# The first run of matmuls takes six weight tiles instead of four, with its weights loaded chunk by chunk into three raw buffers

## The reference

```python
def rmsnorm(x, g):
    xf = x.astype(jnp.float32)
    y = xf * lax.rsqrt(jnp.mean(xf * xf, axis=-1, keepdims=True) + EPS)
    return (y * g.astype(jnp.float32)).astype(x.dtype)

def swiglu(x, w_gate, w_up, w_down):
    return (jax.nn.silu(x @ w_gate) * (x @ w_up)) @ w_down

def first_block(x, meta_tokens, ffn1_norm, ffn1_w_gate, ffn1_w_up, ffn1_w_down, ...):
    meta = jnp.broadcast_to(meta_tokens.astype(x.dtype)[None], (B, N_META, D_MODEL))
    h = jnp.concatenate([meta, x], axis=1)
    for l in range(DEPTH):
        h = h + 0.5 * swiglu(rmsnorm(h, ffn1_norm[l]), ffn1_w_gate[l], ffn1_w_up[l], ffn1_w_down[l])
        proj = rmsnorm(h, mix_norm[l]) @ w_in[l]
        ...                                     # retention and differential attention, w_out
        h = h + 0.5 * swiglu(rmsnorm(h, ffn2_norm[l]), ffn2_w_gate[l], ffn2_w_up[l], ffn2_w_down[l])
    h = rmsnorm(h, final_norm)
    return h[:, N_META:]

# second_block: SwiGLU, short convolution, SwiGLU, SwiGLU, dilated attention, SwiGLU, each behind an rmsnorm
```

## Time and profile before

| | |
|---|---|
| median of three runs | 2173.55 us (2172.53 to 2174.04) |
| the profiled execution | 2174.74 us |
| its span, first to last instruction | 2172.9 us |
| TensorE busy | 2161.8 us, 99% of the span |
| VectorE busy | 1558.9 us, 72% |
| ScalarE busy | 1221.3 us, 56% |
| GpSimd busy | 461.5 us, 21% |
| chain that ended last | TensorE 92%, DVE 4%, ACT 2%, DMA 1%, issue 1% |
| mean granted TensorE clock | 0.948 |

### The profile page before, as it was taken

The page is one execution under the profiler, slowest core; times in us unless marked ns, Lnnn a source line. Parts: engine busy times, 40 slices in busy tenths (PEclk is TensorE's granted clock), DMA queues, the critical chain, the costliest instruction groups (busy, mean ns, idle before and its releaser), DMA issues.

```text
span 2172.9 us, 38658 instructions
## 1 busy us (share of the span) xinstructions
PE 2161.8 (99%) x15616; PEld 2040.9 (94%) x15616; DVE 1558.9 (72%) x2589; ACT 1221.3 (56%) x2020; POOL 461.5 (21%) x500
## 2 busy tenths in 40 slices
PE   9999999999999999999999999999999999999999
PEld 9999999999999999988988999889888999999888
DVE  7655876765665586886697586975876688887863
ACT  6444465544544446665566545654655666676652
POOL 1000522420341052232053000430321011101420
PEclk9999999999999999999999999999999999999999
DMA  9655434975785543565566554755565566674653
GB/s 277 202 170 171 155 121 133 235 197 174 190 213 175 183 156 117 163 206 184 165 211 199 191 179 152 233 185 191 186 194 175 170 194 171 175 236 139 225 178 105
DMA packets 425680, 395.34 MB, mean 182 GB/s; under 512 B 16559, under 2 KB 421935, under 8 KB 425504
## 3 DMA queue, kind: packets, MB, share of 16 engines
q1 hardware_dynamic: 411856, 375.01, 55.3%
q0 software_dynamic: 13360, 17.61, 3.9%
q10 hardware_dynamic: 288, 0.27, 0.0%
HBM read 389.20 MB, written 7.41 MB: 183 GB/s over the span
## 4 chain that ended last, share of the span: by engine, by line
PE 92%; DVE 4%; ACT 2%; DMA 1%; issue 1%; SPq 0%; DVEq 0%; ACTq 0%
PE ps L1663 29%; PE ps L1659 25%; PE ps L1661 16%; PE ps L1662 16%; DVE t L1155 2%; PE ps L1982 1%; PE ps L1980 1%; PE ps L1981 1%; DMA t<-attn_w_qkv 1%; ACT t L830 0%; PE ps L1948 0%; PE ps L1932 0%; PE ps L1961 0%; DMA t<-ffn_w_up 0%; PE ps L1758 0%
## 5 line engine op out<-in xcount | busy, mean ns | idle before, releaser
L1663 PE MATMUL ps<-t 128*128 128x256 f32 (+1 forms) x5504 | 1562.2, 284 | 0.0
L1663 PEld LDWEIGHTS ps<-t 128*128 128x128 f32 x5504 | 1038.4, 189 | 0.1
L1155 DVE TENSOR_TENSOR t<-t 128x1024 fp32r<-128x1024 f32 (+1 forms) x724 | 879.0, 1230 | 175.8 <-ACT t L830 175.3
L1661 PE MATMUL ps<-t 128*128 128x272 f32 (+1 forms) x3084 | 890.3, 289 | 1.0 <-DVE t L1618 0.8
L830 ACT ACTIVATE t<-t 128x1024 fp32r<-128x1024 f32 (+1 forms) x724 | 732.1, 1030 | 265.8 <-PE ps L1663 234.4
L1662 PE MATMUL ps<-t 128*128 128x272 f32 (+1 forms) x3084 | 879.8, 285 | 0.0
L1659 PE MATMUL ps<-t 128*128 128x512 f32 x2420 | 840.4, 390 | 0.1
L1661 PEld LDWEIGHTS ps<-t 128*128 128x128 f32 x3084 | 580.9, 188 | 7.6 <-issue 3.9
L1662 PEld LDWEIGHTS ps<-t 128*128 128x128 f32 x3084 | 583.7, 189 | 1.0
L1659 PEld LDWEIGHTS ps<-t 128*128 128x128 f32 x2420 | 454.2, 188 | 95.3 <-DVE t L1155 0.4
L754 POOL TENSOR_TENSOR t<-t 128x256 f32<-128x256 f32 x110 | 100.2, 910 | 694.0 <-ACT t L946 694.0
(11 more groups left out here) (198 smaller groups left out, 1535.3 us busy)
## 6 DMA issues: line engine op xcount, KB each, us to landing
t<-ffn_w_in SPq DMA_DIRECT2D x88, 1024.0 KB, 5.4
t<-ffn_w_gate SPq DMA_DIRECT2D x42, 1024.0 KB, 5.5
t<-ffn_w_up SPq DMA_DIRECT2D x42, 1024.0 KB, 7.4
t<-attn_w_qkv SPq DMA_DIRECT2D x72, 512.0 KB, 5.0
t<-ffn_w_down SPq DMA_DIRECT2D x32, 1024.0 KB, 5.3
t<-ffn_w_out SPq DMA_DIRECT2D x32, 1024.0 KB, 5.3
t<-w_in SPq DMA_DIRECT2D x28, 1024.0 KB, 5.1
t<-ffn_w_down SPq DMA_DIRECT2D x16, 768.0 KB, 4.4
```

Source lines behind the costliest of these rows:

```text
L1155: dve.tensor_tensor(wlo[:, plan.place[n], 0:nk, :], raw[:, u % NRAW, 0:nk, half * P:half * P + P], f32(whi[:, plan.place[n], 0:nk, :]), AL ...
L1661: pe.matmul(o, hi, xhi, start=i == 0, stop=False)
L1663: ins = pe.matmul(o, lo, xhi, start=False, stop=i == r.nk - 1)
```

## The change

The first run takes six tiles. Its weights are two units of 384 columns, gate and up. They lie in raw buffers 0 to 2, which are seen as eight chunks of 768 columns, and are loaded chunk by chunk with the residual: 24 loads on SP in the place of 13. The two units behind them (tiles 6 and 7) are 128 columns wide and share raw buffer 3. The gains of stage 0 (eight columns) come by a small load of their own ahead of the rest of `vec`. GpSimd loads no part of `h`. DVE makes the high x of chunk 0, ACT that of the other seven, and the two tables of `vec` are made behind all of this. TensorE has its own procedure for the first run (`project_first`): for chunk 0 it does the high by high matmuls of all six tiles, then high by low, then low by high, each group behind its own semaphores; for each other chunk three matmuls a tile as before. Each tile of the run reports its own end (`spent`). The matmul of the norm stays ahead of chunk 5 of the run behind the first, which is now that of tile 6 and was that of tile 4. TensorE does four matmuls without use in the place of five.

```diff
-FIRST = [(0, 1), (1, 2), (2, 4), (4, 6), (6, 8)]
-WARM = 5
+NFIRST = 6
+WARM = 4
...
-                for n in [4] + [1] * (2 * FCH - 4):
+                n = 4 if s else NFIRST
+                for n in [n] + [1] * (2 * FCH - n):
                     self.run(s, n, KC, c0, range(8))
...
+        cols = range(0, F, PAIR)
+        if not self.order:
+            each = NFIRST // 2
+            firsts = [self.unit(w, 0, 8, first, each * P) for w, first in (gate, up)]
+            self.order += [(u, i) for i in range(each) for u in firsts]
+            self.order += [(self.unit(w, 0, 8, first + each * P, P), 0) for w, first in (gate, up)]
+            cols = range(each * P + P, F, PAIR)
+        for c in cols:
+            self.weights_pair(gate[0], gate[1] + c, up[0], up[1] + c)
...
-            self.spent += [mm + i + 1 if i < r.rounds - 1 else mm + i + n] * n
+            last = [mm + 1 + j for j in range(n)] if first == 0 else [mm + i + n] * n
+            self.spent += [mm + i + 1] * n if i < r.rounds - 1 else last
...
+        raw_first = raw[:, 0:3, :, :].rearrange("p r k n -> p (r k n)").rearrange(
+            "p (k u c) -> p k u c", k=KC, u=2)
...
+        def kept(u):
+            if u < NRAW:
+                return raw[:, 3, :, (u - 2) * P:(u - 1) * P]
+            return raw[:, u % NRAW, :, :]
...
             load_first(sp, 0, 1)
-            sp.dma_start(vec[:, :], A["vec"]).then_inc(S["vec"], 16)
...
+            sp.dma_start(vec[:, V_FFN1:V_FFN1 + KC], A["vec"][:, V_FFN1:V_FFN1 + KC]).then_inc(S["gains"], 16)
+            for k in range(1, KC):
+                load_residual(sp, k)
+                load_first(sp, k, 0)
+                load_first(sp, k, 1)
+                if k == 2:
+                    sp.dma_start(vec[:, KC:], A["vec"][:, KC:]).then_inc(S["vec"], 16)
...
                 if u >= NRAW:
-                    w.wait_ge(S["lo"], plan.last[u - NRAW] + 1)
+                    w.wait_ge(S["lo"], max(plan.last[u - NRAW] + 1, NFIRST))
...
+            w.wait_ge(S["gains"], 16)
+            for k in range(KC):
+                if k:
+                    high_x(0, k)
+                w.wait_ge(S[f"first{k}"], 32)
+                ins = act.activation(first_pieces(whi, k), first_pieces(raw, k), ACT.Copy)
+                ins.then_inc(*((S["hi_first"], 1) if k < KC - 1 else (S["hi"], NFIRST)))
+            hi.up(NFIRST)
             w.wait_ge(S["vec"], 16)
             w.wait_ge(S["set"], 1)
...
+            w.wait_ge(S["gains"], 16)
+            w.wait_ge(S["h0"], 16)
+            dve.tensor_scalar(x[:, 0, 0, :], h[:, 0, :], gain(0, 0), None, ALU.mult).then_inc(S["xh"], 1)
+            for k in range(KC):
+                low_x(0, k)
+                w.wait_ge(*((S["hi_first"], k + 1) if k < KC - 1 else (S["hi"], NFIRST)))
+                ins = dve.tensor_tensor(first_pieces(wlo, k), first_pieces(raw, k), f32(first_pieces(whi, k)), ALU.subtract)
...
+            def project_first(r):
+                def product(part, k, j):
+                    wt, m = ((whi, 0), (whi, 1), (wlo, 0))[part]
+                    return pe.matmul(ps[:, r.banks[j], 0:T], wt[:, plan.place[j], k, :], x[:, k, m, :],
+                                     start=(part, k) == (0, 0), stop=(part, k) == (2, KC - 1))
+                for part, sems in enumerate((("xh", "hi_first"), ("xl",), ("lo_first",))):
+                    for name in sems:
+                        w.wait_ge(S[name], 1)
+                    for j in range(r.n):
+                        product(part, 0, j)
+                for k in range(1, KC):
+                    w.wait_ge(S["xl"], k + 1)
+                    w.wait_ge(*((S["lo_first"], k + 1) if k < KC - 1 else (S["lo"], NFIRST)))
+                    for j in range(r.n):
+                        for part in range(3):
+                            ins = product(part, k, j)
+                        if k == KC - 1:
+                            ins.then_inc(S["mm"], 1)
...
-                project(runs[0], None if late else normed(s, 6))
-                for r in runs:
+                if s == 0:
+                    project_first(runs[0])
+                else:
+                    project(runs[0], None if late else normed(s, 6))
+                for r in runs[1:]:
                     t = r.first - T0[s]
...
-                    project(r, normed(s, 1 if s else 5) if late and t == 4 else None)
+                    project(r, normed(s, 1 if s else 5) if late and r is runs[1] else None)
```

More of the change, by code:

```diff
@@ L416 @@
 SEMS = (
-    [f"raw{i}" for i in range(NRAW)] + [f"{name}{i}" for name in ("first", "h") for i in range(len(FIRST))]
-    + ["vec", "square", "squares", "init", "const", "scr", "bands", "bias0", "bias1", "out"]
+    [f"raw{i}" for i in range(NRAW)] + [f"{name}{i}" for name in ("first", "h") for i in range(KC)]
+    + ["gains", "vec", "square", "squares", "init", "const", "scr", "bands", "bias0", "bias1", "out"]
     + ["hi", "lo", "warm", "hi_first", "lo_first", "mm", "evac", "set"]
@@ L578, in made @@
             if e == 0:
-                return S[f"h{[m < end for _, end in FIRST].index(True)}"], 16
+                return S[f"h{m}"], 16
             return S["evac"], T0[e] - KC + m + 1
@@ L829, in highs @@
                         w.wait_ge(S["mm"], plan.spent[plan.prev[n]])
-                    act.activation(whi[:, plan.place[n], 0:nk, :], raw[:, u % NRAW, 0:nk, half * P:half * P + P],
+                    act.activation(whi[:, plan.place[n], 0:nk, :], kept(u)[:, 0:nk, half * P:half * P + P],
                                    ACT.Copy).then_inc(S["hi"], 1)
@@ L1123, in _ @@
             log_exp()
+            w.wait_ge(S["gains"], 16)
[6 more added lines that the diff above has]
+            hi.up(NFIRST)
             w.wait_ge(S["vec"], 16)
             w.wait_ge(S["set"], 1)
[L1126 to L1129, removed]
-                for k in range(k0, k1):
-                    ins = act.activation(first_pieces(whi, k), first_pieces(raw, k), ACT.Copy)
-                    ins.then_inc(*((S["hi_first"], 1) if k < KC - 1 else (S["hi"], 4)))
-            hi.up(4)
             for m in range(KC):
                 if m == 4:
-                    highs(4)
+                    highs(NFIRST)
                 squared(0, m)
@@ L1154, in lows @@
                     w.wait_ge(S["hi"], n + 1)
-                    dve.tensor_tensor(wlo[:, plan.place[n], 0:nk, :], raw[:, u % NRAW, 0:nk, half * P:half * P + P],
+                    dve.tensor_tensor(wlo[:, plan.place[n], 0:nk, :], kept(u)[:, 0:nk, half * P:half * P + P],
                                       f32(whi[:, plan.place[n], 0:nk, :]), ALU.subtract).then_inc(S["lo"], 1)
@@ L1606, in _ @@
             own.up()
+            w.wait_ge(S["gains"], 16)
[5 more added lines that the diff above has]
+                ins = dve.tensor_tensor(first_pieces(wlo, k), first_pieces(raw, k), f32(first_pieces(whi, k)), ALU.subtract)
+                ins.then_inc(*((S["lo_first"], 1) if k < KC - 1 else (S["lo"], NFIRST)))
+            lo.up(NFIRST)
             w.wait_ge(S["vec"], 16)
@@ L1612, in _ @@
             w.wait_ge(S["set"], 1)
-            for k0, k1 in FIRST:
-                for k in range(k0, k1):
-                    low_x(0, k)
-                for k in range(k0, k1):
-                    w.wait_ge(*((S["hi_first"], k + 1) if k < KC - 1 else (S["hi"], 4)))
-                    ins = dve.tensor_tensor(first_pieces(wlo, k), first_pieces(raw, k), f32(first_pieces(whi, k)), ALU.subtract)
-                    ins.then_inc(*((S["lo_first"], 1) if k < KC - 1 else (S["lo"], 4)))
-            lo.up(4)
             for m in range(KC):
                 if m == 4:
-                    lows(4)
+                    lows(NFIRST)
                 added(0, m)
```

33 lines of the change are left out of this document (11 added, 22 removed).

## The result

The changed kernel takes 2179.69 us (median of eleven runs, 2178.18 to 2181.3) against 2173.55 for the kernel before (eleven runs, 2171.62 to 2177.18). The ratio is 1.0028, 95% interval 1.002 to 1.0035: slower by 6.1 us, where 5.1 was forecast. The profiled execution took 2179.69 us, its span 2177.7.

The account below looks back on a forecast made before the run. TensorE, busy 2161.8 of 2172.9 us, was taken to bound the kernel. Tile 7's later start, +3.8 (the start's gain included), and the clock, +1.4, gave +5.2, carried as +5.1: 2173.55 + 5.1 = 2178.7 us, range 2176.2 to 2181.0.

Parts of the forecast that it names:

- The wait for tile 7: Behind tile 6, TensorE stands still 4.95 us for tile 7's low part, at the end of the norm's chain.
- Two counts: Matmuls counted in the kernel before: 54 from the norm to tile 7, 30 to the end of the first 144.
- The start: First run: first matmul at 5.25, 1.05 us earlier; six tiles end at 24.45; -1.2 us, bounds 0 to -2.
- the wait at chunk 1: In the first run, TensorE waits for chunk 1's weights: 0.2 us allowed, bounds 0 to 1.0.
- the half pace at the start: First matmuls of the first run go at half pace: 0.9 us lost against 0.5 before, bounds 0.5 and 1.5.
- Tile 7's start: Tile 7 begins at 32.9 where it was 29.1, 3.8 us later, and this stays to the end.
- The clock: Behind the wait for tile 7 the granted clock falls to 0.50, costing 1.4 us, bounds 0 and 3.0.
- A: Rival: tile 7 is late but the clock holds or falls under a microsecond; +3.8, 2177.3 us; chance 0.13.
- B: Rival: tile 7 is not late, only the start counts; -1.2, 2172.3 us; chance 0.08.
- C: Rival: low clock lasts longer, up to 3.0 us, or the start is held up; +6.8, 2180.4; with D 0.11.
- D: Rival: the loads bind the first run, SP's 24 small loads keeping the rate low; +6, 2179.7; with C 0.11.

Follow-up runs that it names:

- the wait filled: The changed kernel with 42 matmuls without use on TensorE between tile 6 and its wait for tile 7: 2176.98 us, ratio 1.0015.
- the cured kernel: The changed kernel, but tiles 7 and 8 are made ahead of the norm's root and the norm's matmul stands ahead of chunk 1 of tile 6: 2172.27 us.
- a four-tile run: The changed kernel with a first run of four tiles, 256 columns a unit, and tiles 4 to 7 in units of 128: 2176.06 us, ratio 1.0013.
- the kernel before once more: The kernel before, unchanged, profiled one more time in one execution: 2173.75 us, span 2171.9.
- the kernel before with the norm moved: The kernel before with the norm's matmul of stage 0 ahead of chunk 5 of tile 6, not of tile 4: 2180.5 us, ratio 1.0032.
- high x by ACT: The changed kernel, but ACT and not DVE makes the high x of chunk 0, ahead of its high weights: 2180.71 us, one execution.

## Why the prediction was right, step by step

**The wait for tile 7** was the main term and holds: 4.95 us foretold, for the low part of tile 7, once. Tile 7 could have begun at 28.37, one matmul's pace behind the last of tile 6 (28.24), and began at 33.42: 5.05 us. (The profile's 4.89 is counted from the modelled end of that matmul.) The step was read from the order (9 matmuls between norm and tile 7 in the place of 57) and the length of a chain which nobody had to wait for before. Three experiments fix it: the same wait in the kernel before by moving the norm alone, the wait gone by making the tiles ahead of the root, and the wait shorter by what the norm is moved.

**Two counts** in the forecast are wrong by three matmuls. Behind the norm's matmul stand nine of tile 4 and not six, 57 up to tile 7 and not 54, and to the 144th it is 33 and not 30. The forecast also counted from 22.33, the modelled end of the norm's matmul, which is later than the spacing of the starts gives, and this hid most of the error by luck. The timeline of the kernel before has tile 7 at 29.30 and not 29.1, and tile 6, the end of the first 144 matmuls, at 26.29, less 0.47 for the norm's matmul 25.82 and not 25.65. Its 0.8 us to spare were thus about 0.9.

**The start** was sized too well. The sixth tile was to end at 24.45; measured 24.90. Against 25.82 the start gained 0.9 us. Of the 0.45 that are missing, 0.2 is the first matmul at 5.47 and not 5.25: ACT's release is the gains' small load, at 4.49, in the step that I had put at 4.3, and the load of `h` came at 4.75, not 4.55. 0.3 is the wait at chunk 1, 0.48 and not 0.2; the half pace at the start took about 0.8 and not 0.9. ACT's 768 columns took 0.84 (0.83 taken as the middle), DVE's 0.95 (0.96).

**Tile 7's start** follows: 33.42 and not 32.9, 5.05 - 0.93 = 4.1 us later than before and not 3.8.

**The clock** fell in the wait as forecast, and cost 1.8 us and not 1.4. The stretch taken as its measure was 15 matmuls at the slow pace; here there were 18 until it was back. The term was mis-sized, within its bounds. The Trainium skill's page weighed for it, "TensorE: Matmul & The Clock Gate", section "HAM oscillation — how this bites in real kernels", tells of waits between bursts of matmuls that send the engine back to half clock. The trace agrees: a wait in the middle of dense work brought the next matmuls to half clock, at 4.9 us of wait and also at 3.4.

**Rivals.** A (the clock holds) is refuted for waits of 4.9 us: it fell in all three profiles with such a wait, and the mean clock of 0.998 stands in all eleven executions of the changed kernel. With the wait filled, the clock did hold. B (the start decides) describes the kernel in which tile 7 is cured: 2172.27 where B said 2172.3. That they agree to the tenth is luck, since the interval is 3.7 us wide. C's longer fall and D's starved loads did not show; no chunk but chunk 1 waits. What neither the forecast nor a rival had seen is that the new start costs a four-tile run 2.9 us (2176.06 against 2173.2), at least half of it because the squares and tile 4's load stand behind it. The six tiles hide just that. I put the cost of these two at nothing and named the run's length as the cover, and that was right; without it they would have been late.

What stays open: whether the cured kernel gains anything. 0.9995 (0.9986 to 1.0003) is -1.1 us with an interval that holds zero. The timeline has tile 7 at 28.22 against 29.30, -1.1. But behind 1700 us TensorE's waits sum to 4.6 us in the cured kernel's profile and to 3.3 in that of the kernel before once more, and its span is only 0.7 us shorter, though it also lacks the fall in the light stretch (1.4 us). With one profile each it is not shown whether that late loss comes from the change.

## What to carry to other kernels

A group of work that is made longer takes cover away from whatever stands at a fixed place behind it: count the instructions between the place where a long chain starts and the place where its result is wanted, in the order before and after. A chain that shows no wait may have little to spare (here 0.9 of 6.0 us); its length is read from its links on the other engines, not from the waits. And a wait of a few us in dense matmul work costs more than its length: here 4.9 us took another 1.8 through the clock, while work whose inputs had long been ready (tile 7's) stood in the queue behind the chain.

## What the runs showed of the hardware

- Waits of 4.9 and 3.4 us brought the granted clock to 0.50, and it came back some 4 to 5 us after the work had begun again. The matmuls up to then took 1.8 us more than at full pace in the changed kernel, 2.4 in the kernel before with the norm moved, 2.2 with high x by ACT (all 4.9 us of wait) and 1.6 at 3.4 us. A wait of 2.8 us, 2 us of matmuls behind one of 1.6, brought it too, but the mean clock says not in every execution; waits of 2.3, 0.85 and 0.5 us did not. With 42 dummy matmuls in the gap it stayed at 1.00.
- A light stretch (the eight small matmuls of the earlier trace rows) brought 0.50 in six of twelve profiles and not in the other six.
- At the start the granted clock reads 1.00 in the window from 6 to 7 us, while the matmuls in it stand 0.23 us apart (6.67, 6.90, 7.13 on the timeline). There the pace is read from the starts and not from this column.
- A profile may read a granted clock of 0.95 throughout while the matmuls of 272 columns keep their 0.126 us; the same kernel read 1.00 another time, with a span 1.0 us shorter. Its ordinary fp32 matmuls of 256 columns (L1961) took 388 ns at 0.95 and 379 at 1.00 (median).
- The landing of the same 192 KB load varied by 0.76 us between kernels with the same start (6.71 to 7.47), nearly the whole gain of the start (0.9).
